# Residual and bias loads move from GpSimd's queue to SyncE's, and the last output tile is finished in two column pieces

## The reference, cut to what matters

```python
x = x + mixed @ w_out[layer]                         # kept in DRAM as dX1
...
y = lax.map(expert_block, ...)                       # act @ w_down[e] + b_down[e]
y = y * buf_w[:, None]                               # gate of each (token, expert)
out = jnp.zeros((n_tok, d)).at[buf_tok].add(y)
x = x + out
```

## Time and profile before

| | us |
|---|---|
| median of 3 runs | 2281.24 |
| profiled execution, own time | 2280.05 |
| its span | 2278.4 |
| first DMA of the last stage (POOL, bias) | at 2205.66 |
| first pick issued | at 2208.66 |
| last addition begins | at 2272.89 |
| last store issued | at 2274.14 |

### The profile page before, as it was taken

The page is one execution under the profiler, slowest core; times in us unless marked ns, Lnnn a source line. Parts: engine busy times, 40 slices in busy tenths (PEclk is TensorE's granted clock), DMA queues, the critical chain, the costliest instruction groups (busy, mean ns, idle before and its releaser), DMA issues.

```text
span 2278.4 us, 38736 instructions
## 1 busy us (share of the span) xinstructions
PE 2143.4 (94%) x11173; PEld 1818.9 (80%) x11174; DVE 1576.3 (69%) x2058; ACT 1288.3 (57%) x1653; POOL 617.9 (27%) x648
## 2 busy tenths in 40 slices
PE   7999998899995999999999999999999999999965
PEld 5877777655885899889998898998787998798952
DVE  4455653632337678888778877778888778977766
ACT  4255343445233566676666766666777666767650
POOL 2015663134432112232112212112232212322125
PEclk9999998899996999999999999999999999999987
DMA  4234455503245679899778978879999879979789
GB/s 148 95 96 110 136 142 169 179 28 102 105 176 194 232 249 323 296 373 325 251 252 306 368 249 274 292 251 339 383 372 379 275 255 352 379 270 344 256 277 372
DMA packets 308105, 568.13 MB, mean 249 GB/s; under 512 B 35708, under 2 KB 64892, under 8 KB 308052
## 3 DMA queue, kind: packets, MB, share of 16 engines
q1 hardware_dynamic: 294756, 520.13, 67.3%
q0 software_dynamic: 13296, 47.32, 5.3%
HBM read 508.03 MB, written 57.51 MB: 248 GB/s over the span
## 4 chain that ended last, share of the span: by engine, by line
PE 61%; DVE 3%; POOL 2%; issue 1%; DMA 1%; DVEq 0%; ACT 0%; POOLq 0%; ACTq 0%
PE banks L2456 17%; PE banks L206 10%; PE banks L208 10%; PE banks L207 10%; PE banks L2458 7%; PE banks L2394 2%; PE banks L2393 2%; DVE VL L1230 2%; PE banks L1250 1%; PE banks L2455 1%; POOL yk L2172 1%; PE banks L2398 1%; DMA yk<-dY,pos 1%; DVE u L2307 1%; DVE A L2278 1%
## 5 line engine op out<-in xcount | busy, mean ns | idle before, releaser
L1230 DVE TENSOR_TENSOR VL<-RAW,VH 128x2048 fp32r<-128x2048 f32 x389 | 883.9, 2285 | 78.2 <-ACT VH L1225 69.5
L1225 ACT ACTIVATE VH<-RAW 128x2048 fp32r<-128x2048 f32 x390 | 730.7, 1908 | 48.0 <-PE banks L208 48.0
L2456 PE MATMUL banks<-T,VH 128*128 128x384 f32 x1920 | 545.3, 359 | 18.6 <-POOL hot_e L2122 13.3
L2458 PE MATMUL banks<-T,VL 128*128 128x192 f32 x1680 | 422.5, 252 | 0.0
L2456 PEld LDWEIGHTS banks<-T,VH 128*128 128x128 f32 x1920 | 346.8, 190 | 22.6 <-issue 22.3
L2458 PEld LDWEIGHTS banks<-T,VL 128*128 128x128 f32 x1680 | 322.6, 192 | 0.2
L206 PE MATMUL banks<-VH,A 128*128 128x512 f32 x512 | 209.3, 409 | 6.2 <-DVE A L2278 4.5
L206 PE MATMUL banks<-VH,T 128*128 128x512 f32 x544 | 211.9, 390 | 0.0
L207 PE MATMUL banks<-VL,T 128*128 128x512 f32 x544 | 211.9, 390 | 0.0
L208 PE MATMUL banks<-VH,T 128*128 128x512 f32 x544 | 211.8, 389 | 0.0
L208 PE MATMUL banks<-VH,A 128*128 128x512 f32 x512 | 200.4, 391 | 0.0
(11 more groups left out here) (369 smaller groups left out, 3846.2 us busy)
## 6 DMA issues: line engine op xcount, KB each, us to landing
RAW<-in_expert_w_gate_up SPq DMA_DIRECT2D x528, 512.0 KB, 5.0
RAW<-in_expert_w_down SPq DMA_DIRECT2D x262, 512.0 KB, 6.9
RW<-in_w_in SPq DMA_DIRECT2D x24, 512.0 KB
dY<-zeros SPq DMA_DIRECT2D x17, 512.0 KB
dY<-yb SPq DMA_DIRECT2D x68, 128.0 KB, 8.1
dY<-yb SPq DMA_DIRECT2D x32, 256.0 KB, 7.4
xin<-in_x SPq DMA_DIRECT2D x8, 512.0 KB, 9.8
MBC<-dM SPq DMA_DIRECT2D x8, 512.0 KB, 11.1
```

Of the source, the lines that this page charges most:

```text
L1225: act.activation(VH[:, i, ks], RAW[:, i, ks], ACT.Copy).then_inc(s_hi, 1)
L1230: dve.tensor_tensor(VL[:, i, ks], RAW[:, i, ks], VH[:, i, ks].bitcast(f32), ALU.subtract).then_inc(s_w, 1)
L2456: last = pe.matmul(o[:, 0:2 * NW], VH[:, c % 3, k, col], T2[:, k], start=k == 0, stop=k == KT - 1)
L2458: pe.matmul(o[:, HI_ALL], VL[:, c % 3, k, col], T2[:, k, HI_ALL], start=False, stop=False)
```

## The change

SP issues the residual loads and the three bias loads, in this order: residual 0, the biases, residual 1, and from there residual t + 2 ahead of the store of tile t - 1. They stand in SP's program behind its loop. POOL issues picks alone. In the last tile VectorE adds the banks after picks 1 and 2, and the last pick in two pieces of 512 columns; each piece is stored by a DMA of its own.

```diff
@@ block.sync
                 n = superblocks(sp, narrow, wide)
-                for t in range(TT):
-                    sp.wait_ge(s_xb, t + 1)
-                    sp.dma_start(out2[tok(t), :], acc[:, t]).then_inc(s_sent, 16)
-                sp.wait_ge(s_sent, 16 * TT)
+
+                def residual(t):
+                    sp.dma_start(acc[:, t], dX1[tok(t), :]).then_inc(s_x1[t % 2], 16)
+
+                wait(s_hi, n * N2 + 6)
+                wait(s_w, n * N2 + 5)
+                residual(0)
+                for g in range(3):
+                    sp.dma_start(bdr[NE * g:NE * g + NE], b_dn).then_inc(s_bd, 16)
+                residual(1)
+                for t in range(TT - 1):
+                    if t + 2 < TT:
+                        sp.wait_ge(s_x1[t % 2], 16 * (t // 2 + 1))
+                        residual(t + 2)
+                    if t >= 1:
+                        sp.wait_ge(s_xb, t)
+                        sp.dma_start(out2[tok(t - 1), :], acc[:, t - 1]).then_inc(s_sent, 16)
+                sp.wait_ge(s_xb, TT - 1)
+                sp.dma_start(out2[tok(TT - 2), :], acc[:, TT - 2]).then_inc(s_sent, 16)
+                for j in range(2):
+                    sp.wait_ge(s_xb, TT + j)
+                    sp.dma_start(out2[tok(TT - 1), j * CH:(j + 1) * CH], acc[:, TT - 1, j * CH:(j + 1) * CH]).then_inc(s_sent, 16)
+                sp.wait_ge(s_sent, 16 * (TT + 1))
@@ block.gpsimd
-                for g in range(3):
-                    pool.dma_start(bdr[NE * g:NE * g + NE], b_dn).then_inc(s_bd, 16)
-                residual(0)
-                residual(1)
...
-                    if t + 2 < TT:
-                        pool.wait_ge(s_x1[t % 2], 16 * (t // 2 + 1))
-                        residual(t + 2)
@@ block.vector
-                    for k in range(1, TOPK):
+                    for k in range(1, TOPK if t < TT - 1 else TOPK - 1):
...
-                    dve.tensor_tensor(acc[:, t], acc[:, t], pair(t % 3, D), ALU.add).then_inc(s_xb, 1)
+                    if t < TT - 1:
+                        dve.tensor_tensor(acc[:, t], acc[:, t], pair(t % 3, D), ALU.add).then_inc(s_xb, 1)
+                last, k = TT - 1, TOPK - 1
+                dve.tensor_tensor(acc[:, last], acc[:, last], pair(last % 3, D), ALU.add).then_inc(s_sum, 1)
+                dve.wait_ge(s_sum, (TOPK - 1) * TT)
+                dve.wait_ge(s_picked[last % YR][k], 16 * (last // YR + 1))
+                for j in range(2):
+                    cols = slice(j * CH, (j + 1) * CH)
+                    dve.scalar_tensor_tensor(out=acc[:, last, cols], in0=yk[:, last % YR, k, cols], scalar=g4[:, last, k:k + 1], in1=acc[:, last, cols],
+                                             op0=ALU.mult, op1=ALU.add).then_inc(s_xb, 1)
```

More of the change, by code:

```diff
@@ L2154, in _ @@
                 wait(s_xg[1], n * 16 + 16)
-                def residual(t):
-                    pool.dma_start(acc[:, t], dX1[tok(t), :]).then_inc(s_x1[t % 2], 16)
                 wait(s_hi, n * N2 + 6)
                 wait(s_w, n * N2 + 5)
-                for g in range(3):
-                    pool.dma_start(bdr[NE * g:NE * g + NE], b_dn).then_inc(s_bd, 16)
-                residual(0)
-                residual(1)
                 for i in range(2):
```

## The result

The changed kernel took 2294.27 us (median of 6 runs, 2289.83 to 2297.93), the kernel before 2281.14 (6 runs). The ratio is 1.0062, 95% interval 1.0049 to 1.0074: a loss of 13.1 us. Forecast were 2284.8, range 2280.8 to 2288.9. The direction was right, the size was not: the forecast was a loss too small to be told from none, and the prediction had left 0.40 for a clear one. The profiled execution took 2297.93 us, its span is 2296.2.

The account below looks back on a forecast made before the run. The last stage was taken as bound by DMA bytes; 4.1 us of new DMA idle time less 0.5 us at the last tile made +3.6, giving a forecast of 2284.8 us, range 2280.8 to 2288.9.

Parts of the forecast that it names:

- Bytes bind: Last stage, 2207 to 2271: DMA share about 1.0 at 406 to 415 GB/s, so only DMA idle time moves the end.
- The hole: DMA engines idle around the 17th pick, near 2237 to 2242: 4.1 us, bounds 0 and 8.2.
- slow packets: Bias loads: their packets move 262 GB/s instead of 410, 0.7 us lost.
- POOL's earlier start: Start of the picks: first pick near 2206.8, 1.9 us earlier, priced at nothing; at most a gain of 1.9 us.
- The chain biases, `bd3`, PE, gate, 17th pick, hole: Biases land 2232.5, `bd3` 2234.8, PE finishes tile 0 at 2239.4, 17th pick 2239.7, DMA engines then idle: +4.1 us.
- gate: The moment PE has done tile 0, freeing buffers for the 17th pick; forecast at 2239.4.
- The tail: Last tile: split third product +0.10 us, smaller last store saves 0.64 us; sum -0.5 us.
- the first step of SP's part: SP after its empty turns: leaves its loop at 2223.4, first DMA at about 2223.8.
- SP comes later still: Rival: another 1.9 us of stalls in SP's empty turns delays biases, PE and picks; +5.5, 2286.7 us; chance 0.40.
- The upper bound of 8.2 us: Most DMA idle time: 4.1 plus SP stalls 1.9, slower biases 0.4 and later first pick data 1.8.
- The loads are quick: Rival: biases land 3 us earlier, DMA idle only 1.2 us; sum +0.7, 2281.9 us; chance 0.10.

Follow-up runs that it names:

- after_turns: The changed kernel with every engine's loop run n times instead of 53, so without the 21 empty turns; 2281.27 us, ratio 1.0010.
- held: The changed kernel with POOL waiting for residual 0 to land before its first pick; 2295.16 us, ratio 1.0058.
- same4: The changed kernel unaltered, run again on another chip; 2287.74 us, ratio 1.0020.
- run 32: Not a follow-up run: these words only say that the loop's bodies run 32 times, its working turns; no kernel and no measured time belong to them.
- lean: The kernel before with the last tile in two pieces, no empty turns and no test of s < n; 2280.00 us, ratio 0.9990.
- later4: later_only unaltered, run again on another chip; 2280.58 us, ratio 0.9988.
- later_only: The changed kernel with biases and residuals 0 and 1 back on POOL's queue, residuals 2 to 7 on SP's; 2280.09 us, ratio 0.9998.

## Why the prediction was wrong

Right, point by point, the first of them in part only:
- *Bytes bind.* The hole is in the trace: no hole with after_turns, 11.7 us in the changed kernel, 10 us and more in another place in held. But "the end can move only by the time in which the 16 DMA engines become idle" was right in part only. Counted over the whole stage in windows of 1 us, all engines together stand idle for 7.4 us before, 19.6 in the changed kernel and 10.2 in same4, where no turn is stretched. The rest, stage time less idle time less the stage's bytes (27.8 to 28.0 MB) at 412 GB/s, a rate between those of the earlier trace rows, is time in which they are busy but slow: 1.6, 4.7 and 4.1 us. So of the changed kernel's 15.6 us about 12.2 are idle time and 3.1 slow transfers, and of same4's 5.2 about 2.8 and 2.5. Two windows of same4, the biases and residuals beside the picks, then the hole:
```profile
2230.00:2236.00 6.00, 0.00 (x0) 0.00 (x0) 0.00 (x0) 0.00 (x0) 1.11 (x2) 0.50 1.03 323
2240.00:2246.00 6.00, 6.00 (x11) 2.64 (x10) 5.03 (x5) 0.00 (x0) 1.72 (x2) 0.62 0.67 255
```
  The prediction had 0.7 us for slow packets and took 410 GB/s for all else.
- *POOL's earlier start is worth nothing.* The first pick came 6.0 us after the last store's issue instead of 6.9, on the landing of that store (I had said 5.0), and no trace gained from it.
- *The chain biases, `bd3`, PE, gate, 17th pick, hole.* Every link stands in the trace. same4 even has its length up to the 17th pick. From the last store's issue my 17th pick was at 2239.7 - 2201.79 = 37.9 us, and same4 has 2243.98 - 2205.98 = 38.0:
```profile
2225.71 0.35 SPq L2104 DMA_DIRECT2D acc<-dX  x1
2236.14 1.06 ACT L2279 ACTIVATE bd<-bdr 96x1024 fp32r<-96x1024 f32 x1 [14.72 <-DMA bdr<-in_expert_b_down]
2243.98 0.95 POOL L2184 DMA_INDIRECT yk<-dY,pos  x1 [12.56 <-PE banks L2512]
```
  That agreement is luck, errors cancel in it: SP came 2.3 us sooner than in the earlier trace rows, from SP's first load to `bd` it took 10.4 us instead of 8.7, and from `bd` to the pick 7.8 instead of 7.2. The loss there was 5.2 to 5.4 us for my 3.6, and its hole was 2.0 us (share 0.67 in 6 us) instead of my 4.1: the slow transfers made up for it.
- *The tail.* DVE's last three products and the sum take 5.30 us (from 2287.26 to 2292.56) instead of 5.18, and from DVE's end to the end of the span 3.64 instead of 4.29: -0.53, forecast -0.5.
```profile
2287.26 2.61 DVE L2378 SCALAR_TENSOR_TENSOR acc<-yk,g,acc 128x1024 f32<-128x1024 f32 x2 [0.44 <-DMA yk<-dY,pos]
2289.90 1.22 DVE L2385 TENSOR_TENSOR acc<-acc,banks 128x1024 f32<-128x1024 f32 x1
2291.15 1.41 DVE L2390 SCALAR_TENSOR_TENSOR acc<-yk,g,acc 128x512 f32<-128x512 f32 x2
2291.93 0.99 SPq L2123 DMA_DIRECT2D out<-acc  x2
```

Wrong was the first step of SP's part: "SP leaves its loop at 2223.4". It left at 2238.6, or, counted from the last store's issue, 34.6 us after it instead of 21.5. The stage came out 15.6 us longer instead of 3.6, and step by step the 12.0 us between them are, to a tenth:
- SP's exit, 34.6 instead of 21.5: +13.1.
- From SP's first load to `bd` 5.8 us instead of 8.7, as it went out on idle engines: -2.9.
- From `bd` to the 17th pick 7.8 instead of 7.2: +0.6.
- From there to the end of the span 43.5 instead of 42.3: +1.2. The first packet of the 17th pick came 2.4 us after its issue instead of 1.8, and the engines were slow at first.

The rival "SP comes later still" named this mechanism; what failed was its price. I allowed as much stalling again as I took the earlier trace rows to have, 1.9 us (by the 14.6 us of the undisturbed chips it was 2.3), and the argument against it, "SP's turns are the same code as before, under the same full engines, so their time should repeat", was the error: SP's loop was the same and the engines no fuller (share 0.90 from 2212 to 2216, 1.03 from 2224 to 2230), and the time did not repeat. The upper bound of 8.2 us was built on that 1.9 and so did not hold the result. The row that could have warned was there: a loop that takes 17.0 us where 22 quiet tests would span about 15 shows that something outside the program's instructions reaches into it, and how far that goes with another load isn't in the trace.

On the rival "The loads are quick": what it takes from the Trainium skill stands on the page DMA: Bandwidth & Descriptors, about 0.6 us to the first byte under Latency and other measured facts, SP for plain loads under Issuing engine by pattern. In the changed kernel's trace SP's first load, on idle engines, had its first packet 0.99 us after its issue (2239.03 to 2240.02); in same4, beside the picks, it took 3.5 us (2225.71 to 2229.19), as I had forecast from the earlier trace rows.

What stretches the turns is open. Shown is: it comes with the new order, and only on some of the chips (or occasions). It hits SP, DVE and, less, ACT, from about the time when the picks' data flow, in steps of 0.70 us, and ends about when they end; POOL, which is through its own empty turns before the picks start, is untouched. The kernels in which POOL's queue carries the residuals between the picks have little of it there, 2.3 to 2.5 us on SP. That the picks cause it is the likely reading and not a shown one, as held never ran on a chip that stretches. The Trainium skill (Runtime: NRT & Kernel Launch, Instruction fetch mechanics) says that a taken branch whose target lies outside the two pages of code at hand forces a fetch through the engine's own DMA queue, "an ifetch stall". An empty turn jumps over both bodies, so this could be the way in which full DMA engines reach the sequencers. No run separates it. The list of DMA queues from 2200 to 2240 of the changed kernel shows only q0 and q1 and no packet of an instruction queue; but it shows none from 800 to 2200 either, while the loop's bodies run 32 times, so its silence says little. The stalls fall on tests and register moves as well as on branches.

## What to carry to other kernels

A transfer that is moved to another queue starts when that engine's program gets there: read how far behind the engine is, empty loop turns included, before anything is counted of the queue itself. If a stretch of sequencer work (loop tests, branches) carries stalls in the trace, its duration is no constant, and its upper bound must be measured, on more than one chip. Full DMA engines are not always fast ones: count the bytes of each window, not only its busy share. And where executions scatter by more than the effect, a stage time from one event of the trace to the end told in one run what the medians of ten did not.

## What the runs showed of the hardware

- SP's 22 tests of its empty turns span 14.6 us in every trace on two chips, and on the three others 17 or 30 us, by the kernel's order of loads. Whether it is the chip or the occasion isn't separated, as no chip was used twice.
- Under such stalls a single register operation or branch takes 0.70 us, about fourteen to twenty times its usual 0.03 to 0.05.
- With a busy share of 1.0 the 16 DMA engines moved 406 to 415 GB/s in the long windows of the earlier trace rows, but 323 GB/s from 2230 to 2236 in same4, where biases and residuals ran beside the picks.
- Taking the empty turns away (about 15 us of sequencer time on SP, DVE and ACT each) gained nothing in the kernel before (stage time 76.8 against 76.4 to 76.6): they lay beside transfers that the stage was busy with.
- No version is clearly faster than before. lean has a ratio of 0.9990 (0.9981 to 0.9999), a gain at the edge of what can be measured and not in this stage (76.8 us); later4 has 0.9988 with an interval that reaches 1.0002, and its first run, later_only, 0.9998.
